# Mixers' gates moved by DMA and transposed on TensorE as fp32r instead of float32

## The chip, the cores and the metric

The kernel runs on one core of a Trainium2 chip. A core has five engines with instruction queues of their own, which run in order and wait for each other through semaphores: TensorE (PE in the profile; its weight loads are PEld), VectorE (DVE), ScalarE (ACT), GpSimd (POOL) and SyncE (SP). Sixteen DMA engines move data between memories. The metric is the device time of one execution in microseconds.

## What is computed

A stack of two blocks over 256 rows of 1024 columns, all in float32. The first block has two mixers, a sliding window attention and a block attention; the second has two hybrid layers. Only the mixers of the first block have the gates that this change touches. A mixer is, cut down:

```python
proj = h @ w_in                                   # q, k, v, z
o = attention(rope(q), rope(k), v)                # softmax(...) @ v
o = o.reshape(B, S, MIX_WIDTH) * jax.nn.silu(z)   # the gate
h = h + o @ w_out[i]
```

## The kernel before

Rows are cut into M = 2 tiles of P = 128; the 1024 columns into KD = 8 tiles of 128. Every weight matrix arrives in chunks of 1 MB (`raw`, three buffers, loaded by SP). ScalarE rounds a chunk to fp32r (`hi`, L1547), VectorE takes the rest (`lo`, L1159), and TensorE multiplies three times, hi by hi, lo by hi and hi by lo (L1371). fp32r is the kind of float32 operand that TensorE takes in one pass. A chunk of 4 x 128 x 512 is 24 products of 128x512. The split of a chunk is queued two chunks ahead of its products.

What each engine does and in which order is one list of steps, made by `build_schedule`; each engine walks it and emits its own part of every step. There is no planner: a step's place in the code is its place in each queue.

A mixer (`mixer_ab`) projects q, k, v, then the two halves of z (512 columns each), then multiplies by `w_out`. Its attention is cut into stages `attention(sc, n)`, n = 0 to 5, laid between the chunks; the names `att(n)` stand for them. Stage 3 has, on ScalarE, the last eight exponentials of the scores (`attn_prob`, L1734 and L1736).

The gate, for each half of z and each m:

- `ev_z` (ScalarE, L1657) makes silu(z) from PSUM as `attn_z`. `den` (VectorE) makes 1 / softmax sum, `dens`.
- `gate` (GpSimd, L1901) multiplies both into `quarter`, 128 x 512 in float32. There are two quarter buffers, shared with other work.
- `turn_gate` (TensorE, L1250) transposes the quarter as four blocks of 128x128 into a PSUM bank (`bank<-cst,quarter`; `cst` holds the identity), since the attention's result `attn_o` stands transposed. VectorE multiplies `attn_o` by it (L2243).
- `split_o` rounds the product into `oT_hi` (ScalarE, L1769) and `oT_lo` (VectorE, L2248), from which the output product reads.

So there are 2 mixers x 2 halves x 2 row tiles = 8 quarters and 32 transposes of this kind. Half 0's two quarters are turned together, in the middle of the second chunk of z's second half. Half 1's are turned singly, in the middle of the first and of the second chunk of the output product.

`turn_gate` and `split_o` of both halves are called here:

```python
b = halves(sc, w_in, [(D + 2 * kvw + 512, 512)], [lambda: fill_gates(sc, a, 0, za)], att(3),
           [lambda: turn_gates(sc, a, 0)])
...
out_product(sc, w_out, KD, {
    0: (att(5), [lambda: turn_gates(sc, a, 1, 0)]),
    1: ([lambda: turn_gates(sc, a, 1, 1)], ())}, mid)
```

Of the kernel before, what the change touches and what calls it, by code (L numbers as in the profile page):

```python
# [22 lines left out]
F32 = mybir.dt.float32  # L23
F32R = mybir.dt.float32r
# [6 lines left out]
S, D, P = 256, 1024, 128  # L31
# [397 lines left out]
def halves(sc, w, cols, a=(), b=(), c=()):  # L429

    blk = sc.block(sum(cw for _, cw in cols))
    project_chunk(sc, w, cols, [0, 1, 2, 3], blk, True, False, a, b)
    project_chunk(sc, w, cols, [4, 5, 6, 7], blk, False, True, c)
    return blk
# [75 lines left out]
def fill_gates(sc, a, half, z):  # L510


    es = a["sinks"][half] if a["kind"] == "a" else None
    den = sc.step("den", att=a, half=half, es=es)
    a["gates"][half] = [sc.quarter("gate", att=a, half=half, m=m, z=z, den=den) for m in range(M)]


def turn_gates(sc, a, half, *ms):


    turned = []
    for m in ms or range(M):
        b = sc.bank()
        oev = a["oev"][2 * half:2 * half + 2]
        s = sc.step("turn_gate", att=a, half=half, m=m, of=a["gates"][half][m], oev=oev, bank=b)
        b.freed = (s, "vector")
        sc.turned_quarter(s)
        turned.append(s)
    for s in turned:
        sc.oturned[half, s.m] = sc.step("split_o", att=a, half=half, m=s.m, of=s)  # L530


def new_attention(sc, which, heads, nkv):
    a = sc.att = {"kind": which, "heads": heads, "nkv": nkv, "scores": [], "flip": [], "pv": [], "oev": [],
                  "base": sc.heads, "tk": [], "tq": [], "gates": {}, "sinks": [], "normed": {}}
    sc.heads += heads
    if which == "h" and sc.heads == 40:
        sc.prob_readers, sc.last_pv4 = [None] * 4, [None] * 2
    return a


def mixer_ab(sc, which, w_in, w_out, nkv, mid=False):

    kvw = nkv * HD
    a = new_attention(sc, which, 16, nkv)

    def att(*ns):
        return [lambda n=n: attention(sc, n) for n in ns]

    kv = [(D, 2 * kvw)]  # L550
    b = halves(sc, w_in, [(0, 512)])
    ev = evacs(sc, b, "ev_q", j=0, kind_of=which)
    rq0 = sc.step("pool_rope" if nkv > 2 else "rope_q", j=0, kind_of=which, ev=ev)
    if nkv == 2:
        b = sc.block(2 * kvw)
        project_chunk(sc, w_in, kv, list(range(KD)), b, True, True)
    else:
        b = halves(sc, w_in, kv)
    ev = evacs(sc, b, "ev_kv", nkv=nkv, dt=None)
    kr = sc.step("rope_k", nkv=nkv, kind_of=which, ev=ev)  # L560
    if sc.heads == 32:

        bk = sc.bank()
        s = sc.step("taps", bank=bk)
        bk.freed = (s, "scalar")
    b = halves(sc, w_in, [(512, 512)], (), [lambda: turn_queries(sc, a, 0, rq0)], [lambda: turn_keys(sc, a, kr)])
    ev = evacs(sc, b, "ev_q", j=1, kind_of=which)
    rq1 = sc.step("pool_rope", j=1, kind_of=which, ev=ev)
    sc.low_later = True
    sc.goes_on(att(0))  # L570

    def queries():
        turn_queries(sc, a, 1, rq1)
        if mid:
            sc.step("mid_load", before=a["tq"][-1])

    b = halves(sc, w_in, [(D + 2 * kvw, 512)], (), att(1), [queries])
    sc.goes_on(att(2))
    za = evacs(sc, b, "ev_z", j=0, kind_of=which)
    if mid:  # L580
        sc.gain_now = sc.gain(None)
        sc.gain_now["made"] = sc.step("mid_gain")
    b = halves(sc, w_in, [(D + 2 * kvw + 512, 512)], [lambda: fill_gates(sc, a, 0, za)], att(3),
               [lambda: turn_gates(sc, a, 0)])
    sc.goes_on(att(4))
    zb = evacs(sc, b, "ev_z", j=1, kind_of=which)
    fill_gates(sc, a, 1, zb)
    out_product(sc, w_out, KD, {
        0: (att(5), [lambda: turn_gates(sc, a, 1, 0)]),
        1: ([lambda: turn_gates(sc, a, 1, 1)], ())}, mid)  # L590


# [313 lines left out]
def half_of(c, half):  # L906
# [13 lines left out]
    "scores": ("tensor", "vector", "scalar"),   # L920
    "flip4": ("tensor", "vector"), "scalar_flip4": ("tensor", "scalar"), "pv4": ("tensor",),
    "oev4": ("scalar",), "vector_oev4": ("vector",), "o_split": ("scalar", "vector"), "over": ("vector",),
    "p_norm_scalar": ("scalar",), "p_norm_vector": ("vector",), "sink": ("vector", "scalar"), "den": ("vector",), "gate": ("gpsimd",),
    "turn_gate": ("tensor", "vector"), "split_o": ("scalar", "vector"), "pool_rope": ("gpsimd",),
    "soft1": ("vector", "scalar"), "soft2": ("vector", "scalar"), "soft3": ("vector",),
    "sums": ("tensor", "vector", "scalar"), "conv": ("tensor", "scalar", "vector"), "conv_silu": ("scalar",),
# [10 lines left out]
def build(nc, t):  # L937
# [14 lines left out]
    def at(name, shape, dt, where=None):  # L952
        size = math.prod(shape[1:]) * (2 if dt == BF16 else 4)
        size = -(-size // LINE) * LINE
        if where is None:
            where = place[0]
            place[0] += size
        else:
            at.end = max(at.end, where + size)
        return nc.alloc_sbuf_tensor_at(name, shape, dt, offset=where), where + size  # L960

    def keep(name, shape, dt=F32):
        return at(name, shape, dt)[0]
# [6 lines left out]
    warm, _ = at("warm", [P, 1], BF16, place[0] - 2 * 12 * S * 4)  # L970
    gain_rows8, _ = at("gain_rows8", [KD, P], F32, place[0] - 2 * 12 * S * 4 + 1024)
    gain_cols, _ = at("gain_cols", [P, KD], F32, place[0] - 2 * 12 * S * 4 + 1536)
    raw = [keep(f"raw{i}", [P, CH]) for i in range(RAW)]
    hi = [keep(f"hi{i}", [P, CH], F32R) for i in range(SPLIT)]
    lo = [keep(f"lo{i}", [P, CH], F32R) for i in range(SPLIT)]
# [113 lines left out]
    taps_in, e = at("taps_stage", [P, P], F32, e)  # L1089
    angle, e = at("trig_stage", [P, M, 2, 8], F32, e)  # L1090
    sine, e = at("trig_stage2", [P, M, 2, 8], F32, e)
    turns, _ = at("trig_stage3", [P, M, 2, 8], F32, e)

    mid_rows = [at(f"mid_row{i}", [P, D], F32, A["q_at"] + 4 * D * i)[0] for i in range(2)]
    assert max(place[0], at.end) <= 229344, (place[0], at.end)
# [21 lines left out]
    warm_up = nc.alloc_semaphore("warm_up")  # L1117
    picks_made = nc.alloc_semaphore("picks_made")
    gain_in = nc.alloc_semaphore("gain_in")
    setup_dve = nc.alloc_semaphore("setup_vector")  # L1120
    setup_act = nc.alloc_semaphore("setup_scalar")
    out_done = [nc.alloc_semaphore(f"out_done{m}") for m in range(M)]
# [3 lines left out]
    def ended(eng, step, who):  # L1126

        eng.wait_ge(sem[step.kind, who], step.i + 1)
# [119 lines left out]
    def _(pe):  # L1248
# [26 lines left out]
        for s in sc.steps:  # L1275
# [184 lines left out]
                                                pt[:, p0 + r * QC + S:p0 + r * QC + QC], start=False, stop=True)  # L1460
                last.then_inc(sem["pv4", "tensor"], 1)
            elif s.kind == "turn_gate":
                ended(pe, s.of, "gpsimd")
                bank = freed(pe, s.bank)
                for i in range(4):
                    last = transpose(bank[:, i * P:(i + 1) * P], quarter[s.of.buf][:, i * P:(i + 1) * P])
                last.then_inc(sem["turn_gate", "tensor"], 1)
            elif s.kind == "sums":
                ended(pe, s.before, "vector")
# [69 lines left out]
    def _(act):  # L1539
# [38 lines left out]
        for s in sc.steps:  # L1578
# [12 lines left out]
            elif s.kind == "turn":  # L1591
                act.wait_ge(sem["turn", "tensor"], s.i + 1)
                bank = psum[4 + s.bank.at]
                if s.dst == "h":
                    out = hT[0][:, s.k0:s.k0 + 2, :].rearrange("p k t -> p (k t)")
                    done(nc.scalar.activation(out, bank[:, :], ACT.Copy), s)
                else:
                    dst = (xT if s.dst == "x" else oT)[0]
                    done(nc.scalar.activation(dst[:, s.k0:s.k0 + 4, s.m * P:(s.m + 1) * P],
                                              bank[:, :].rearrange("p (k t) -> p k t", k=4), ACT.Copy), s)  # L1600
            elif s.kind == "piece":
                piece(s.i)
            elif s.kind == "x_split":
# [805 lines left out]
```

## Time and profile before

| | us |
|---|---|
| median of 3 runs | 851.33 |
| range of the runs | 851.17 to 851.60 |
| profiled execution, its time | 851.23 |
| profiled execution, its span | 849.4 |

Busy shares of the span: TensorE 99%, VectorE 74%, ScalarE 63%, GpSimd 24%. The granted clock of TensorE is at full speed over the whole span. The span is the stretch from the first to the last instruction; 1.8 us of the execution's time lie around it.

### The profile page before, as it was taken

The numbers are of one execution on the slowest core, as the hardware profiler recorded it, in microseconds if no ns is written. First come the engines' busy times: TensorE is split into PE (matmuls) and PEld (weight loads), VectorE is DVE, ScalarE is ACT, GpSimd is POOL, SyncE is SP. The second block draws the span as 40 slices with busy tenths as digits, with TensorE's granted clock in tenths as the row PEclk, the third lists the DMA queues.
The fourth block names the chain that finished last, engine by engine and source line by source line (L and its number), as shares of the span: only waits on it lengthen the run. The fifth ranks groups of instructions, "written<-read, shape, count | busy, mean of one in ns | idle before, by whom it ended". The sixth has DMA issues, their size and how long they took to land.

```text
span 849.4 us, 13003 instructions
## 1 busy us (share of the span) xinstructions
PE 842.3 (99%) x4635; PEld 707.1 (83%) x4635; DVE 624.3 (74%) x1109; ACT 535.6 (63%) x1035; POOL 202.3 (24%) x175
## 2 busy tenths in 40 slices
PE   9999999999999999999999999999999999999997
PEld 6888888788888888888888888888888888888885
DVE  6867865778776798688888546576797688888544
ACT  8677466856896864655556434787874655665533
POOL 0221053110152420033333000152330043334000
PEclk9999999999999999999999999999999999999999
DMA  9823563446534435665655565444347566565631
GB/s 329 287 82 124 174 204 117 150 149 188 172 119 146 149 131 192 206 199 182 186 194 196 200 198 175 152 148 149 104 145 222 176 198 198 184 181 185 227 116 50
DMA packets 94307, 146.20 MB, mean 172 GB/s; under 512 B 5924, under 2 KB 54564, under 8 KB 94244
## 3 DMA queue, kind: packets, MB, share of 16 engines
q1 hardware_dynamic: 92212, 139.58, 50.1%
q0 software_dynamic: 1296, 4.72, 1.6%
q10 hardware_dynamic: 736, 1.07, 0.3%
q8 instruction: 38, 0.62, 0.3%
q14 instruction: 25, 0.20, 0.1%
HBM read 144.32 MB, written 1.05 MB: 171 GB/s over the span
## 4 chain that ended last, share of the span: by engine, by line
PE 99%; DMA 0%; ACT 0%; DVE 0%; SPq 0%; issue 0%; DVEq 0%; ACTq 0%
PE bank L1371 58%; PE bank L1324 17%; PE bank L1327 9%; PE bank L1250 6%; PE bank L1528 2%; PE bank L1456 1%; PE bank L1432 1%; PE bank L1429 1%; PE bank L1459 1%; PE bank L1271 0%; PE bank L1266 0%; DMA h<-in_x 0%; PE bank L1518 0%; PE bank L1535 0%; PE bank L1269 0%; PE bank L1496 0%
## 5 line engine op out<-in xcount | busy, mean ns | idle before, releaser
L1159 DVE TENSOR_TENSOR lo<-raw,hi 128x1024 fp32r<-128x1024 f32 x242 | 308.8, 1293 | 106.3 <-ACT hi L1547 106.0
L1547 ACT ACTIVATE hi<-raw 128x1024 fp32r<-128x1024 f32 (+1 forms) x258 | 269.3, 1061 | 138.1 <-PE bank L1371 70.8
L1371 PE MATMUL bank<-hi,xT 128*128 128x512 f32 (+2 forms) x800 | 251.9, 386 | 0.0
L1371 PEld LDWEIGHTS bank<-hi,xT 128*128 128x128 f32 x800 | 147.2, 188 | 30.8 <-issue 4.3
L1371 PE MATMUL bank<-lo,xT 128*128 128x512 f32 (+2 forms) x400 | 151.1, 378 | 0.0
L1324 PE MATMUL bank<-xT,hi 128*128 128x512 f32 x640 | 149.5, 390 | 0.0
L1324 PEld LDWEIGHTS bank<-xT,hi 128*128 128x128 f32 x640 | 118.7, 188 | 24.3 <-DVE quarter L2143 0.5
L1371 PE MATMUL bank<-hi,hT 128*128 128x512 f32 x348 | 107.7, 389 | 0.0
L1371 PEld LDWEIGHTS bank<-lo,xT 128*128 128x128 f32 x400 | 75.4, 189 | 12.1
L1327 PE MATMUL bank<-xT,lo 128*128 128x256 f32 x640 | 80.5, 283 | 0.0
L1327 PEld LDWEIGHTS bank<-xT,lo 128*128 128x128 f32 x640 | 79.4, 191 | 1.4
L1371 PEld LDWEIGHTS bank<-hi,hT 128*128 128x128 f32 x348 | 65.3, 188 | 13.5
L1371 PE MATMUL bank<-lo,hT 128*128 128x512 f32 x174 | 67.7, 389 | 0.0
L1371 PE MATMUL bank<-hi,oT_hi 128*128 128x512 f32 x160 | 66.1, 413 | 0.0
L1859 POOL TENSOR_TENSOR f_up<-f_up,row_scale 128x256 f32<-128x256 f32 x40 | 46.4, 1182 | 73.3 <-DVE f_up L2154 73.3
L1371 PE MATMUL bank<-hi,oT_lo 128*128 128x512 f32 x160 | 62.6, 391 | 0.0
L1371 PE MATMUL bank<-lo,oT_hi 128*128 128x512 f32 x160 | 62.4, 390 | 0.0
L1159 POOL TENSOR_TENSOR lo<-raw,hi 128x1024 fp32r<-128x1024 f32 x16 | 39.0, 2445 | 61.4 <-ACT hi L1547 61.4
L1859 POOL TENSOR_TENSOR f_gate<-f_gate,row_scale 128x256 f32<-128x256 f32 x40 | 33.9, 869 | 79.2 <-DVE f_gate L2154 79.2
L2302 DVE SCALAR_TENSOR_TENSOR hyb_acc<-bank,taps,hyb_acc 128x255 f32<-128x255 f32 (+2 forms) x72 | 29.0, 474 | 15.8 <-ACT hyb_acc L1794 15.8
L1371 PEld LDWEIGHTS bank<-lo,hT 128*128 128x128 f32 x174 | 32.7, 188 | 6.8
L1371 PEld LDWEIGHTS bank<-hi,oT_hi 128*128 128x128 f32 x160 | 30.1, 188 | 6.7 <-issue 1.3
(285 smaller groups left out, 1085.2 us busy)
## 6 DMA issues: line engine op xcount, KB each, us to landing
raw<-in_w_in SPq DMA_DIRECT2D x26, 1024.0 KB, 5.0
raw<-in_w_down SPq DMA_DIRECT2D x22, 1024.0 KB, 4.9
raw<-in_w_out SPq DMA_DIRECT2D x20, 1024.0 KB, 5.1
raw<-in_w_gate SPq DMA_DIRECT2D x20, 1024.0 KB, 5.3
raw<-in_w_up SPq DMA_DIRECT2D x20, 1024.0 KB, 5.3
raw<-in_w_in_b SPq DMA_DIRECT2D x10, 1024.0 KB, 5.0
raw<-in_w_in_a SPq DMA_DIRECT2D x7, 1024.0 KB, 7.7
raw<-in_w_in_a SPq DMA_DIRECT2D x8, 256.0 KB, 5.3
```

What stands on the lines that cost most here:

```text
L1159: return engine.tensor_tensor(lo[r][:, cols], raw[c.i % RAW][:, cols], hi[r][:, cols].bitcast(F32), ALU.subtract)
L1250: return nc.tensor.transpose(out, in_, ident)
L1324: last = nc.tensor.matmul(both, hi[r][:, still], xx[:, k, :, :], start=first, stop=last_one, skip_group_check=c.i % 2 == 1)
L1327: last = nc.tensor.matmul(bank[:, 0:S], lo[r][:, still], xT[0][:, k, :], start=first, stop=last_one, skip_group_check=c.i % 2 == 1)
L1371: last = nc.tensor.matmul(bank[:, 0:wd], still[a], mv[r][:, off:off + wd], start=c.first and i == 0 and j == 0, stop=(c.last or c.closes a ...
L1429: nc.tensor.matmul(bank[:, 0:P], q[r:r + 64, hd // 2, 0:P], k[r:r + 64, kv, 0:P], start=True, stop=True)
L1432: nc.tensor.matmul(bank[:, P:QC], q[r:r + 64, hd // 2, P:S], k[r:r + 64, kv, 0:S], start=True, stop=True).then_inc(sem["scores", "tensor"], 1)
L1456: nc.tensor.matmul(bank[64 * r:64 * r + 64, o0:o0 + S], v[:, 0, kv + r, :], pt[:, p0 + r * QC:p0 + r * QC + S], start=True, stop=False)
L1528: last = nc.tensor.matmul(bank[:, c0:c0 + HD], Hb[f"MT{s.decay.of.i % 4}"][:, i, :], Hb["xg"][:, s.m, hh * HD:(hh + 1) * HD], start=True, ...
L1547: nc.scalar.activation(hi[c.i % SPLIT][:, cols], raw[c.i % RAW][:, cols], ACT.Copy)\
L1859: nc.gpsimd.tensor_tensor(x[:, :], x[:, :], row_scale[:, :], ALU.mult)\
L2302: ins = stt(acc[:, tap:S], x[:, 0:S - tap], cw[:, 3 - tap, ct:ct + 1], acc[:, tap:S], ALU.mult, ALU.add)
```

## The change

A new step `gate_move` stands between `gate` and `turn_gate`. ScalarE's queue waits for the gate of GpSimd and issues a DMA of 256 KB, from the quarter into one of two tiles `moved`, word for word. `moved` is declared fp32r; the DMA goes through a float32 view, so no bit changes. TensorE waits for the landing, and transposes `moved` as fp32r into a bank that is viewed as fp32r, with an identity in fp32r (`same`), which ScalarE makes once, ahead of the first move. `moved` lies in the part of `oT_hi` that the mixers don't use. The moves of half 0 are queued behind attention stage 3, those of half 1 ahead of stage 5.

```diff
+def move_gates(sc, a, half):
+    a["moved"][half] = [sc.step("gate_move", of=a["gates"][half][m]) for m in range(M)]
...
-    b = halves(..., [lambda: fill_gates(sc, a, 0, za)], att(3),
+    b = halves(..., [lambda: fill_gates(sc, a, 0, za)], att(3) + [lambda: move_gates(sc, a, 0)],
                [lambda: turn_gates(sc, a, 0)])
...
-        0: (att(5), [lambda: turn_gates(sc, a, 1, 0)]),
+        0: ([lambda: move_gates(sc, a, 1)] + att(5), [lambda: turn_gates(sc, a, 1, 0)]),
...
             elif s.kind == "turn_gate":
-                ended(pe, s.of, "gpsimd")
+                if s.i == 0:
+                    pe.wait_ge(same_made, 1)
+                pe.wait_ge(gate_moved[s.of.i % 2], 16 * (s.of.i // 2 + 1))
                 bank = freed(pe, s.bank)
                 for i in range(4):
-                    last = transpose(bank[:, i * P:(i + 1) * P], quarter[s.of.buf][:, i * P:(i + 1) * P])
+                    last = nc.tensor.transpose(bank[:, i * P:(i + 1) * P].bitcast(F32R),
+                                               moved[s.of.i % 2][:, i * P:(i + 1) * P], same[:, :])
...
+            elif s.kind == "gate_move":
+                if s.i == 0:
+                    nc.scalar.activation(same[:, :], ident, ACT.Copy).then_inc(same_made, 1)
+                ended(act, s.of, "gpsimd")
+                if s.i >= 2:
+                    act.wait_ge(sem["turn_gate", "tensor"], s.i - 1)
+                act.dma_start(moved[s.i % 2][:, :].bitcast(F32), quarter[s.of.buf][:, :])\
+                   .then_inc(gate_moved[s.i % 2], 16)
```

ScalarE's queue at the end of attention stage 3 of the first mixer (half 0), before. Names are out<-in, the semaphores waited for are in brackets:

```order
L1734 ACTIVATE attn_prob,totals<-bank,shift 128x128 [waits flip4_tensor,scores_vector]
L1736 ACTIVATE attn_prob,totals<-bank,shift 128x256
L1547 ACTIVATE hi_60<-raw_57 128x1024 [waits chunk_tensor,raw_in1]
L1769 ACTIVATE oT_hi<-attn_o 128x4x128 [waits turn_gate_vector] x2
L1547 ACTIVATE hi_60<-raw_57 128x1024
```

The same place in the change:

```order
L1754 ACTIVATE attn_prob,totals<-bank,shift 128x128 [waits flip4_tensor,scores_vector]
L1756 ACTIVATE attn_prob,totals<-bank,shift 128x256
L1615 ACTIVATE same<-cst 128x128
L1619 DMA moved_56<-quarter_67 128x512 [waits gate_gpsimd]
L1619 DMA moved_57<-quarter_68 128x512 [waits gate_gpsimd]
L1559 ACTIVATE hi_62<-raw_59 128x1024 [waits chunk_tensor,raw_in1]
L1789 ACTIVATE oT_hi<-attn_o 128x4x128 [waits turn_gate_vector] x2
L1559 ACTIVATE hi_62<-raw_59 128x1024
```

The two moves stand behind the exponentials and ahead of the split of the next chunk.

TensorE's queue at the turning of half 0, first mixer, before and in the change:

```order
L1371 MATMUL bank<-hi_61,xT 128x512
L1250 MATMUL bank<-cst,quarter_65 128x128 [waits scalar_flip4_scalar,gate_gpsimd]
L1250 MATMUL bank<-cst,quarter_65 128x128 x3
L1250 MATMUL bank<-cst,quarter_66 128x128 [waits flip4_vector,gate_gpsimd]
L1250 MATMUL bank<-cst,quarter_66 128x128 x3
L1371 MATMUL bank<-hi_61,xT 128x512 [waits x_split_vector]
```

```order
L1380 MATMUL bank<-hi_63,xT 128x512
L1477 MATMUL bank<-same,moved_56 128x128 [waits scalar_flip4_scalar,gate_moved0,same_made]
L1477 MATMUL bank<-same,moved_56 128x128 x3
L1477 MATMUL bank<-same,moved_57 128x128 [waits flip4_vector,gate_moved1]
L1477 MATMUL bank<-same,moved_57 128x128 x3
L1380 MATMUL bank<-hi_63,xT 128x512 [waits x_split_vector]
```

The place in the queue is the same; the wait for GpSimd has become one for the landing.

ScalarE's queue at half 1 of the first mixer, before and in the change:

```order
L1547 ACTIVATE hi_61<-raw_58 128x1024 [waits chunk_tensor,raw_in2]
L1752 ACTIVATE attn_o<-bank 128x512 [waits pv4_tensor] x2
L1547 ACTIVATE hi_61<-raw_58 128x1024
L1769 ACTIVATE oT_hi<-attn_o 128x4x128 [waits turn_gate_vector]
```

```order
L1559 ACTIVATE hi_63<-raw_60 128x1024 [waits chunk_tensor,raw_in2]
L1619 DMA moved_56<-quarter_67 128x512 [waits turn_gate_tensor,gate_gpsimd]
L1619 DMA moved_57<-quarter_68 128x512 [waits turn_gate_tensor,gate_gpsimd]
L1772 ACTIVATE attn_o<-bank 128x512 [waits pv4_tensor] x2
L1559 ACTIVATE hi_63<-raw_60 128x1024
L1789 ACTIVATE oT_hi<-attn_o 128x4x128 [waits turn_gate_vector]
```

The copies of `attn_o` and half a split now stand behind two waits for GpSimd.

## Rows read from the trace of the kernel before

**Rows 1.** The page: busy times of the engines, and the chain that ended last.

```profile
PE 842.3 (99%) x4635; PEld 707.1 (83%) x4635; DVE 624.3 (74%) x1109; ACT 535.6 (63%) x1035; POOL 202.3 (24%) x175
...
PE 99%; DMA 0%; ACT 0%; DVE 0%; SPq 0%; issue 0%; DVEq 0%; ACTq 0%
```

**Rows 2.** Timeline of PE, half 0 of both mixers: start, length (us), line, count.

```profile
69.96 1.04 PE L1250 MATMUL bank<-cst,quarter 128*128 128x128 f32 x8
70.75 0.47 PE L1371 MATMUL bank<-hi,xT 128*128 128x512 f32 x1
...
170.56 1.04 PE L1250 MATMUL bank<-cst,quarter 128*128 128x128 f32 x8
171.35 0.47 PE L1371 MATMUL bank<-hi,xT 128*128 128x512 f32 x1
```

**Rows 3.** Timeline of ACT, end of attention stage 3, both mixers.

```profile
70.49 0.24 ACT L1736 ACTIVATION_READ_ACCUMULATOR attn_prob<-bank,shift 128x1 f32 x1
70.58 1.10 ACT L1547 ACTIVATE hi<-raw 128x1024 fp32r<-128x1024 f32 x1
...
171.10 1.10 ACT L1547 ACTIVATE hi<-raw 128x1024 fp32r<-128x1024 f32 x1
```

**Rows 4.** Timeline of POOL, gates of the first mixer, half 0 and half 1.

```profile
62.18 2.06 POOL L1901 TENSOR_TENSOR quarter<-attn_z,dens 128x512 f32<-128x512 f32 x2 [16.76 <-ACT attn_z L1657]
78.88 3.04 POOL L1901 TENSOR_TENSOR quarter<-attn_z,dens 128x512 f32<-128x512 f32 x2 [14.64 <-ACT attn_z L1657]
```

**Rows 5.** DMA issues: tile, queue, count, KB each, median us from issue to landing.

```profile
raw<-in_w_in_b SPq DMA_DIRECT2D x10, 1024.0 KB, 5.0
out<-result SPq DMA_DIRECT2D x3, 256.0 KB, 2.1
raw<-in_w_in SPq DMA_DIRECT2D x2, 64.0 KB, 5.1
```

**Rows 6.** Line L1709, a DMA issued by ACT: the issue's ns, its landing.

```profile
L1709 ACTq DMA_DIRECT2D out<-result x1: 360/360/360, 846.5 to 846.5; - x1
...
DMA to landing us min/median/max: 2.1/2.1/2.1
```

**Rows 7.** Stretches of 1 us: busy us (instructions), clock, DMA share, GB/s.

```profile
71.00:72.00 1.00, 1.00 (x6) 0.79 (x6) 1.00 (x2) 0.68 (x1) 0.00 (x0) 1.00 0.00 0
82.00:83.00 1.00, 1.00 (x6) 0.82 (x5) 0.78 (x1) 0.19 (x1) 0.00 (x0) 1.00 1.07 416
```

**Rows 8.** Groups of PE and PEld by shape: busy us, mean ns | idle before.

```profile
L1371 PE MATMUL bank<-hi,hT 128*128 128x512 f32 x348 | 107.7, 389 | 0.0
L1353 PE MATMUL bank<-hi,hT 128*128 128x256 f32 x8 | 1.6, 282 | 0.0
L1250 PE MATMUL bank<-cst,quarter 128*128 128x128 f32 x152 | 22.4, 272 | 0.0
...
L1371 PEld LDWEIGHTS bank<-hi,hT 128*128 128x128 f32 x348 | 65.3, 188 | 13.5
L1250 PEld LDWEIGHTS bank<-cst,quarter 128*128 128x128 f32 x152 | 18.7, 140 | 4.4
L1528 PEld LDWEIGHTS bank<-hyb_xg,hyb_MT 128*128 128x128 f32 x128 | 15.2, 192 | 0.3
```

**Rows 9.** Timeline of PE: products in bfloat16, and 64-wide ones in float32.

```profile
286.38 0.62 PE L1518 MATMUL bank<-csum,picks 112*128 112x128 bf16 x8
...
289.62 1.89 PE L1528 MATMUL bank<-hyb_xg,hyb_MT 128*128 128x64 f32 x16
```

**Rows 10.** Timelines of PE, ACT and DVE, half 1 of the first mixer.

```profile
83.39 0.60 PE L1250 MATMUL bank<-cst,quarter 128*128 128x128 f32 x4
86.58 0.60 PE L1250 MATMUL bank<-cst,quarter 128*128 128x128 f32 x4
89.79 0.39 PE L1371 MATMUL bank<-hi,oT_hi 128*128 128x512 f32 x1
...
80.64 0.60 ACT L1752 ACTIVATE attn_o<-bank 128x512 f32<-128x512 f32 x1 [0.50 <-PE bank L1459]
...
85.41 0.69 DVE L2248 TENSOR_TENSOR oT_lo<-attn_o,oT_hi 128x512 fp32r<-128x512 f32 x1 [0.70 <-ACT oT_hi L1769]
```

**Rows 11.** PE at the end of the run, and its warm-up at the start.

```profile
843.14 0.28 PE L1353 MATMUL bank<-hi,hT 128*128 128x256 f32 x1
...
847.00:849.40 2.40, 0.00 (x0) 0.57 0.60 212
...
0.93 3.52 PE L1255 MATMUL bank<-warm 128*128 128x512 bf16 x8 [0.93 <-DVE warm L2017]
```

More of the change, by code:

```diff
@@ L524, in turn_gates @@
         oev = a["oev"][2 * half:2 * half + 2]
-        s = sc.step("turn_gate", att=a, half=half, m=m, of=a["gates"][half][m], oev=oev, bank=b)
+        s = sc.step("turn_gate", att=a, half=half, m=m, of=a["moved"][half][m], oev=oev, bank=b)
         b.freed = (s, "vector")
@@ L534, in new_attention @@
     a = sc.att = {"kind": which, "heads": heads, "nkv": nkv, "scores": [], "flip": [], "pv": [], "oev": [],
-                  "base": sc.heads, "tk": [], "tq": [], "gates": {}, "sinks": [], "normed": {}}
+                  "base": sc.heads, "tk": [], "tq": [], "gates": {}, "moved": {}, "sinks": [], "normed": {}}
     sc.heads += heads
@@ L582, in mixer_ab @@
         sc.gain_now["made"] = sc.step("mid_gain")
[L583 removed]
+    b = halves(sc, w_in, [(D + 2 * kvw + 512, 512)], [lambda: fill_gates(sc, a, 0, za)], att(3) + [lambda: move_gates(sc, a, 0)],
                [lambda: turn_gates(sc, a, 0)])
@@ L922 @@
     "oev4": ("scalar",), "vector_oev4": ("vector",), "o_split": ("scalar", "vector"), "over": ("vector",),
-    "p_norm_scalar": ("scalar",), "p_norm_vector": ("vector",), "sink": ("vector", "scalar"), "den": ("vector",), "gate": ("gpsimd",),
+    "p_norm_scalar": ("scalar",), "p_norm_vector": ("vector",), "sink": ("vector", "scalar"), "den": ("vector",), "gate": ("gpsimd",), "gate_move": (),
     "turn_gate": ("tensor", "vector"), "split_o": ("scalar", "vector"), "pool_rope": ("gpsimd",),
@@ L972, in build @@
     gain_cols, _ = at("gain_cols", [P, KD], F32, place[0] - 2 * 12 * S * 4 + 1536)
+    moved = [at(f"moved{i}", [P, 512], F32R, place[0] - (2 * 12 - 8) * S * 4 + 2048 * i)[0] for i in range(2)]
     raw = [keep(f"raw{i}", [P, CH]) for i in range(RAW)]
@@ L1091, in build @@
     sine, e = at("trig_stage2", [P, M, 2, 8], F32, e)
-    turns, _ = at("trig_stage3", [P, M, 2, 8], F32, e)
+    turns, e = at("trig_stage3", [P, M, 2, 8], F32, e)
+    same, e = at("same", [P, P], F32R, e)
     mid_rows = [at(f"mid_row{i}", [P, D], F32, A["q_at"] + 4 * D * i)[0] for i in range(2)]
@@ L1119, in build @@
     gain_in = nc.alloc_semaphore("gain_in")
+    gate_moved = [nc.alloc_semaphore(f"gate_moved{i}") for i in range(2)]
+    same_made = nc.alloc_semaphore("same_made")
     setup_dve = nc.alloc_semaphore("setup_vector")
```

## The prediction, made before the change was run

> **What bounds the kernel now.** I read the page first. TensorE is busy for 842.3 of 849.4 us, and the chain that ended last lies on it for 99% [rows 1]. So every nanosecond of TensorE's own work counts, in both directions, and so does every wait that is put on it: it has no later idle time in which to take a delay back. All other engines have spare time, and what they do counts only where TensorE ends up waiting for it.
>
> Then the timelines, at the places where gates are turned. In half 0 TensorE starts the eight transposes at 69.96 us, and the next product starts at 70.75; in the second mixer these are 170.56 and 171.35 [rows 2]. No idle time stands before either. The gates have long been there: GpSimd starts the first mixer's two at 62.18 and is done after 2.06 us, at 64.24 [rows 4]. The reader should see that this is 5.7 us of slack in front of TensorE, enough for a DMA, if the DMA is issued as soon as the gate is ready. The change doesn't do that. It queues the move on ScalarE behind the last exponentials of attention stage 3, and ScalarE is at them until 70.58 to 70.73 [rows 3], which is after TensorE has arrived at the transposes.
>
> **What the transposes cost, and what is saved.** Eight transposes take 1.04 us, of which the last takes its whole 272 ns: (1.04 - 0.27) / 7 = 0.110 us apart [rows 2, 8]. As fp32r, the product itself should be shorter. A product in fp32r takes 389 ns at 512 columns and 282 at 256, 107 ns for 256 columns or 0.42 ns for one; the float32 transpose of 128 columns takes 272, where this line gives 282 - 54 = 228 [rows 8]. So an fp32r pass streams the identity in about 54 ns, and a float32 transpose in about twice that. The lower end of the spacing is what bfloat16 shows: eight products of 128 columns in 0.62 us, some 0.056 apart [rows 9]. The upper end comes from weight loads. A load in float32 or fp32r for an ordinary product takes 188 to 192 ns, one for a transpose 140 [rows 8]; and 64-wide products, each behind a load of 192 ns, are (1.89 - 0.27) / 15 = 0.108 us apart although they stream only 64 columns [rows 9] (0.27 for the last, as for a transpose). If an fp32r transpose loads its weights like an ordinary fp32r product, it stays at 0.108 and nothing is saved; if it loads like a transpose, it comes to 0.056. I take 0.056, since the load is of a transpose in both kernels and the row of transposes is the nearer one, and keep 0.110 for the range. The saving is 4 x 0.054 = 0.21 us a quarter. For the four quarters of half 1 it is 0.85 us in all, on the path in full. In half 0 it is inside the sum below.
>
> The Trainium skill has a rule that speaks against the change: "TensorE: Matmul & The Clock Gate", Terms, says that trn2's loads and products have a transpose mode which makes float32 4 times faster, so the float32 transpose would already be the quick form. The rows here show a transpose at 272 ns, against 228 for one fp32r pass, so something would be left to save. By the rule alone the saving is nil.
>
> **What the waits cost, half 0.** A move of 256 KB that ScalarE issues costs its queue 0.36 us [rows 6], and 256 KB take 2.1 us from issue to landing [rows 5]. These are writes to memory outside the core, the nearest rows; the moves stay inside. No other traffic is there to disturb them: the DMA engines are idle from 71 to 72 us [rows 7]. 1 MB takes 5.0 us [rows 5], and the engines move about 416 GB/s when busy [rows 7], so 256 KB are 0.64 us of their work. The second move, issued 0.36 us behind the first, lands 0.64 behind it.
>
> - First mixer. ScalarE is free at 70.58 [rows 3]. The identity's copy, once, is 128x128; I put it at 0.25 us. The first move is issued at 70.83 and lands at 72.93; the second lands at 73.57. TensorE turns the first quarter while it waits for the second, then needs 0.05 to notice and 0.22 to turn it. The next product starts at 73.85, not 70.75: +3.1 us.
> - Second mixer. No copy. Issued at 171.10 [rows 3], landings at 173.20 and 173.84, next product at 174.12, not 171.35: +2.8 us.
>
> Together +5.9 us. Behind TensorE nothing gives it back: its wait holds the remaining twelve products of the chunk and all that follows. No row shows a move inside the core, so below the 2.1 I keep an end of 1.4, two thirds of it, with both streams at once: the second landings are then at 72.59 and 172.86, and the stalls 2.1 + 1.8 = 3.9. The page "DMA: Bandwidth & Descriptors" of the Trainium skill, Anatomy of one DMA, gives a fixed 2.0 us plus bytes over 436 GB/s, an estimate of 2.6 us for 256 KB; with it each stall would be 0.5 longer and the time 857.2.
>
> **Half 1.** The gates start at 78.88 and end after 3.04 us, the first near 79.9 and the second at 81.92 [rows 4]. The first move is issued near 79.95, lands near 82.1, and is wanted at 83.39; the second is issued at 81.95, lands near 84.1, and is wanted at 86.58 [rows 10]. No stall, with 1.3 and 2.4 us to spare. What is new is that ScalarE stands in its queue until 81.92. Behind it are the two copies of `attn_o`, of which the second began at 80.64 [rows 10], and half a split of 1.05 us. They would end at about 83.5 and 84.6. VectorE's `oT_lo` for m = 0, which ended at 86.1, then ends near 87.9. The products that read it start at 89.79 [rows 10]. So the delay is hidden by 1.9 us; without that cover it would cost up to the 1.8 us by which `oT_lo` is late, in each mixer. The eight issues (8 x 0.36 = 2.9 us) lie on ScalarE, which is at 63% [rows 1], and for half 0 inside TensorE's stall.
>
> **The sum.** +5.9 (two stalls) - 0.85 (half 1's transposes) = +5.0 us. Against the profiled execution, 851.23 + 5.0 = 856.2; that execution is 0.1 us from the median of the runs.
>
> **The rivals.**
>
> *The transposes don't get faster.* The stalls remain; -0.85 falls away, and in each stall the last quarter takes 0.44 instead of 0.22: +6.3, 857.5. This is also the case in which the change does not do what it says. For it: the skill's rule above, and the loads of 188 ns. Against it: the load's row of 140 for transposes.
>
> *The clock falls in the stalls.* TensorE does nothing for nearly 3 us twice. The trace has one such place, the end of the run: the last product starts at 843.14 and ends at 843.4, and the clock's mean in 847.0 to 849.4 is 0.57 [rows 11], so it fell to the lower level (1.2 GHz) near 847.3, 3.9 us after the last work. That is longer than my stalls, but one case is little. The price: at the start eight products of 512 columns take 3.52 us at the lower level, about 0.42 us each [rows 11], where an fp32r one is 0.23 at the upper; until the clock rises some 1.6 us are lost. With both stalls, +3.2: 859.4.
>
> *The moves of half 1 land late.* A load of 1 MB is under way then: DMA is at 1.07 of its engines in 82 to 83 us [rows 7]. A small transfer queued with a large one took 5.1 us [rows 5]. With that, the first move lands at 85.05 against 83.39, and the same in the second mixer where I allow 1 us: +2.7, 858.9.
>
> *Faster after all.* The mechanism: the wait on the landing costs nothing since the moves are in before TensorE comes, and the transposes' saving is all that is left. The place is half 0 of each mixer. It decides at the issue: the move would have to leave ScalarE before about 67.6 us, 2.1 + 0.2 ahead of 69.96. The gates are there in time [rows 4], but ScalarE's queue runs in order, and the exponentials ahead reach to 70.73 [rows 3]. Price: 8 quarters x 0.21 = 1.7, so 849.5, faster by 0.2%. I see nothing that lets it happen, unless a wait of TensorE elsewhere gives the stalls back; there is none [rows 1].
>
> **How the numbers follow.** Chances: forecast 0.55 (856.2, own range 854.3 to 857.2), transposes not faster 0.2 (857.5), clock 0.12 (859.4), late landings 0.08 (858.9), faster 0.02, and 0.03 for stalls so short that it ends within 0.2%. 0.2%, or 1.7 us, is about what a measurement of this kernel can tell from no change. The range reaches from the short stalls, 851.23 + 3.9 - 0.85 = 854.3, to the clock case, 859.4, with which it takes in the late landings too; only what lies below 854.3 and mixtures of the rivals are left out. Slower by over 0.2% has 0.95.
>
> **What would show it.** Right: TensorE idle for 2.5 to 3 us before the transposes of `moved` in half 0, released by a DMA, twice; none in half 1; eight transposes no longer 0.110 apart; landings 2 to 2.7 us after issues near 70.8 and 171.1 (the second shifted by the first stall). Wrong: a stall in half 1, a granted clock under 1 after a stall, transposes at 272 ns as before, or idle time of TensorE elsewhere, as before the output product's third chunk, where `oT_lo` would be late.

## The result, and the profile after

| | before | after |
|---|---|---|
| median of the runs | 851.47 us (851.17 to 851.64) | 864.67 us (863.0 to 865.04) |
| profiled execution | 851.23 us | 864.48 us |
| its span | 849.4 us | 862.6 us |
| mean granted clock | 0.999 | 0.994 |

The ratio is 1.0152, with an interval of 1.014 to 1.0164: slower by 13.2 us. I had forecast slower by 5.0.

The page of the changed kernel, which answers to [rows 1]: busy times, and the chain that ended last.

```profile
PE 847.6 (98%) x4635; PEld 710.2 (82%) x4635; DVE 624.7 (72%) x1109; ACT 535.2 (62%) x1036; POOL 202.2 (23%) x175
...
PE 95%; DMA 2%; ACT 1%; DVE 0%; issue 0%; POOL 0%; POOLq 0%; ACTq 0%; DVEq 0%
```

Two things stand in it. The chain now passes through DMA and ACT for 3%, so TensorE waits. And TensorE is *busy* for 5.3 us more (847.6 against 842.3) with the same 4635 products. A wait doesn't make products longer; a lower clock does.

The timeline of PE at the four places where it waits. The bracket is the idle time before the group and what ended it.

```profile
71.90 0.50 PE L1477 MATMUL bank<-same,moved 128*128 128x128 f32 x4 [1.73 <-ACT same L1615]
72.60 0.54 PE L1477 MATMUL bank<-same,moved 128*128 128x128 f32 x4 [0.19 <-DMA moved<-quarter]
72.97 0.51 PE L1380 MATMUL bank<-hi,xT 128*128 128x512 f32 x1
...
89.18 0.54 PE L1477 MATMUL bank<-same,moved 128*128 128x128 f32 x4 [1.88 <-DMA moved<-quarter]
...
179.45 0.54 PE L1477 MATMUL bank<-same,moved 128*128 128x128 f32 x4 [1.48 <-DMA moved<-quarter]
180.20 0.54 PE L1477 MATMUL bank<-same,moved 128*128 128x128 f32 x4 [0.21 <-DMA moved<-quarter]
...
195.81 0.60 PE L1477 MATMUL bank<-same,moved 128*128 128x128 f32 x4 [2.48 <-DMA moved<-quarter]
```

The first line names ACT's copy `same`, but that ended at 70.99 (below), 0.9 us earlier. The wait is for several semaphores, and the last to come was the landing of the move. So there are four stalls, not two: half 0 and half 1 of both mixers. Half 1's second quarter (93.98 us) is in time.

Stretches of the same kernel: busy us and count per engine, then the granted clock, DMA share, GB/s.

```profile
71.90:73.00 1.10, 0.91 (x9) 0.77 (x9) 0.56 (x1) 0.03 (x1) 0.00 (x0) 1.00 0.66 84
73.00:76.40 3.40, 3.40 (x11) 2.70 (x10) 2.18 (x4) 2.21 (x3) 0.00 (x0) 0.54 0.79 298
76.40:79.00 2.60, 2.60 (x19) 2.29 (x18) 0.79 (x2) 0.53 (x1) 0.00 (x0) 0.95 0.00 0
...
90.10:93.50 3.40, 3.40 (x10) 2.67 (x9) 2.27 (x3) 1.58 (x2) 0.00 (x0) 0.53 0.81 243
...
180.40:184.00 3.60, 3.60 (x22) 3.06 (x22) 2.34 (x4) 2.22 (x3) 0.00 (x0) 1.00 0.98 263
196.00:199.20 3.20, 3.20 (x11) 2.65 (x11) 2.06 (x3) 1.58 (x2) 0.00 (x0) 0.52 0.94 320
```

After three of the four stalls the clock is at its lower level (1.2 GHz); after the one at 179.45 it stays at 1.00. The count of products shows it too: 11 in 3.4 us there, 22 in 3.6 us here.

**Where the 13.2 us are.** I took the start of a product and subtracted the start of the same product in the trace of before. This difference only moves at these places:

| place | stall | clock after it |
|---|---|---|
| half 0, first mixer | +2.16 | +1.57 |
| half 1, first mixer | +2.05 | +1.58 |
| half 0, second mixer | +1.96 | none |
| half 1, second mixer | +2.68 | +1.54 |
| sum | +8.85 | +4.69 |

The stall is what the difference has gained at the first ordinary product behind the transposes; the clock's part is what it gains after that, until it stands still. The stalls are larger than the brackets, because a product normally starts 0.23 us behind its forerunner, while a bracket counts from the end of the forerunner 0.39 us after its start. The four places give 13.5 us; some 0.3 come back elsewhere, 0.1 of them at half 1's second quarters, where fp32r transposes run without a stall. Behind the last place the difference stays at +13.2 to +13.3 to the end: as good as nothing is given back.

The timeline of ACT and its queue in half 0, which answers to [rows 3]:

```profile
69.40 0.49 ACT L1756 ACTIVATE attn_prob<-bank,shift 128x256 f32<-128x256 f32 x1
69.50 0.51 ACTq L1619 DMA_DIRECT2D moved<-quarter  x1
...
70.06 0.61 ACTq L1619 DMA_DIRECT2D moved<-quarter  x1
...
70.64 0.35 ACT L1615 ACTIVATE same<-cst 128x128 fp32r<-128x128 f32 x1
```

The summary of the tile `moved`, which answers to [rows 6, 8]: ns min/median/max, first and last start, and the landings after their issue.

```profile
L1477 PEld LDWEIGHTS bank<-same,moved x32: 138/140/157, 71.9 to 200.8; 128*128 128x128 f32 x32
L1477 PE MATMUL bank<-same,moved x32: 222/249/308, 71.9 to 200.8; 128*128 128x128 f32 x32
L1619 ACTq DMA_DIRECT2D moved<-quarter x8: 472/473/608, 69.5 to 190.9; - x8
...
DMA to landing us min/median/max: 2.3/3.3/6.9
```

ScalarE issued both moves while exponentials that stand ahead of them in the program were still running, and the first one 1.1 us before the copy `same` began, which also stands ahead of it. That is why half 0's stalls are shorter than forecast. And landings take from 2.3 to 6.9 us: the long ones are half 1's. The chain that ended last, in half 1 of the first mixer (start, length, what), and the load beside it on SP's queue:

```profile
83.75 5.39 DMA moved<-quarter
89.14 0.04 issue
89.18 0.54 PE bank L1477 x4
```

```profile
82.77 7.21 SPq L1224 DMA_DIRECT2D raw<-in_w_in_b  x2
```

The trace's DMA view by queue says how the load holds up the move. In it q1 is SP's queue and q10 is the one of the moves; the numbers are packets, MB and share of the 16 engines. The first line is the stretch from 83.5 to 87.1 us, the other two that from 87.1 to 89.5.

```profile
q1 hardware_dynamic: 449, 0.92, 83.9%
...
q10 hardware_dynamic: 288, 0.52, 57.5%
q1 hardware_dynamic: 79, 0.13, 14.5%
```

The first move is issued at 83.75, but up to 87.1 only the load's packets run: 449 of its 528. Then come both moves together (288 packets) and the load's last 79. In half 0, with no load under way, the packets of a move start 1.2 us behind its issue; here it is 3.4 us. So the engines do not share themselves out between the two: the small transfer stands behind nearly the whole of the large one.

### The profile page after: what moved, and what is told of

The parts are those of the page before. It is cut to its first block, busy times and chain, and to the rows that moved or that the text cites. A ratio compares the mean times of both kernels' runs of the same rounds, so it can differ in the third digit from the quotient of the medians.

```text
span 862.6 us, 13018 instructions
## 1 busy us (share of the span) xinstructions
PE 847.6 (98%) x4635; PEld 710.2 (82%) x4635; DVE 624.7 (72%) x1109; ACT 535.2 (62%) x1036; POOL 202.2 (23%) x175
## 4 chain that ended last, share of the span: by engine, by line
PE 95%; DMA 2%; ACT 1%; DVE 0%; issue 0%; POOL 0%; POOLq 0%; ACTq 0%; DVEq 0%
PE bank L1380 56%; PE bank L1333 17%; PE bank L1336 9%; PE bank L1259 5%; DMA moved<-quarter 2%; PE bank L1540 2%; PE bank L1441 1%; PE bank L1465 1%; PE bank L1438 1%; PE bank L1280 0%; PE bank L1275 0%; PE bank L1530 0%; PE bank L1547 0%; PE bank L1278 0%; PE bank L1264 0%; PE bank L1468 0%
## 5 line engine op out<-in xcount | busy, mean ns | idle before, releaser
L1380 PEld LDWEIGHTS bank<-hi,hT 128*128 128x128 f32 x348 | 65.3, 188 | 13.5
L1380 PE MATMUL bank<-hi,oT_lo 128*128 128x512 f32 x160 | 63.6, 397 | 0.0
L1380 PEld LDWEIGHTS bank<-hi,oT_lo 128*128 128x128 f32 x160 | 30.9, 193 | 6.9
```

What stands on the lines that cost most here:

```text
L1380: last = nc.tensor.matmul(bank[:, 0:wd], still[a], mv[r][:, off:off + wd], start=c.first and i == 0 and j == 0, stop=(c.last or c.closes a ...
```

## The experiments

My theory after this reading had three parts. (1) Half 0 is late because the move is issued late. (2) Half 1 is late because SP's 1 MB load, issued 1 us ahead, holds up the move. (3) TensorE's clock falls after such stalls, at about 1.5 us a time (the expectations below reckon with 1.7). The rivals: ScalarE or its queue is what makes the moves slow; the longer busy time has another cause than the idleness; the fp32r transposes themselves gain or lose more than I think. Line numbers shift by a few between the kernels.

### TensorE kept at work during the wait

```diff
+FILL = 7
...
+    if s.of.i % 2 == 0:
+        for _ in range(FILL):
+            nc.tensor.matmul(bank[:, :], xT[0][:, 0, 0:P], hi[live[0]][:, 0:512], start=True, stop=True)
     pe.wait_ge(gate_moved[s.of.i % 2], 16 * (s.of.i // 2 + 1))
```

> The change, with seven fp32r products of 512 columns (7 x 0.227 = 1.6 us) on TensorE ahead of its wait for the first move of each pair, into the bank that the transposes then overwrite. Theory 1 (13.2 us = about 8 of four stalls plus 5.1 of three falls of the clock, each 3.42 us at the lower level, 1.7 lost): the moves land when they landed, but TensorE isn't idle for them, so the clock stays at 1.00 for the whole span and the time is 864.7 - 5.1 = 859.6. Theory 2 (the slow products after a stall come from something else that the stall brings, such as a loss of order between the queues): the low stretches stay and the time is 864.7 or a little over.

858.60 us (858.55 to 858.77), ratio 1.0085 [1.0069, 1.01]: 6.1 us less than the changed kernel, for extra work on the engine that bounds it. The timeline of PE in half 0:

```profile
70.02 1.75 PE L1477 MATMUL bank<-hi,xT 128*128 128x512 f32 x7
71.96 0.50 PE L1482 MATMUL bank<-same,moved 128*128 128x128 f32 x4 [0.19 <-DMA moved<-quarter]
```

Stretches behind the first mixer's two places and the second's first:

```profile
71.80:75.00 3.20, 2.82 (x17) 2.39 (x18) 2.43 (x4) 1.84 (x4) 0.00 (x0) 1.00 0.70 216
87.00:90.50 3.50, 3.44 (x18) 2.63 (x17) 2.54 (x4) 1.58 (x2) 0.00 (x0) 1.00 0.38 97
175.00:180.00 5.00, 4.71 (x26) 3.70 (x25) 3.58 (x5) 3.34 (x6) 0.00 (x0) 1.00 0.78 280
```

The transposes start no earlier (71.96 against 71.90), but the clock holds at 1.00 where it was 0.53 to 0.54, in these stretches and in all others of the two mixers. This shows part 3: idleness costs clock beyond its own length. Of the 6.1 us 4.7 are the clock's by the table above; the rest is that landings in half 1 took 5.2 us at most instead of 6.9, which this experiment didn't aim at: by the products' offsets half 1's stalls are 1.8 and 1.5 us here, where they were 2.1 and 2.7.

### Each half alone

In both kernels the other half's gates are turned from `quarter` in float32, as before the change. The diff is that of half 0 alone; the other has `half != 1`, and a wait of its moves counts other transposes.

```diff
 def move_gates(sc, a, half):
+    if half != 0:
+        a["moved"][half] = a["gates"][half]
+        return
```

> Only half 0's gates are moved by DMA and turned as fp32r; half 1's as before. Theory 1: the stalls of half 0 alone, 2.2 + 1.9 us, one fall of the clock (1.7) or two (3.4), 16 transposes at 0.085 us apart and not 0.109 (-0.4): 851.4 + 5.4 = 856.8, or 858.5 with two falls. Theory 3 (the four stalls aren't independent, the first one makes the later ones): with half 1 unmoved nearly all of the loss goes, or stays.

> Only half 1's gates are moved by DMA and turned as fp32r; half 0's as before. Theory 1: the stalls of half 1 alone, 2.2 + 2.8 us since the moves land 5 to 7 us after their issue beside a load of 1 MB, two falls of the clock (3.4), 16 transposes at 0.085 us (-0.4): 851.4 + 8.0 = 859.4. The extra of half0 and of this together is that of the change, 13.2. Theory 3 (the stalls of half 1 come from the delay of half 0): no stall here, and 851.0.

Half 0 alone took 855.69 us (855.62 to 855.77), ratio 1.005 [1.0033, 1.0067], with no fall of the clock; half 1 alone 856.91 (856.73 to 857.76), 1.0066 [1.0051, 1.0081], its profiled run the one of 857.76. Half 0 alone, timeline of PE:

```profile
72.41 0.50 PE L1486 MATMUL bank<-same,moved 128*128 128x128 f32 x4 [1.74 <-ACT same L1624]
73.09 0.53 PE L1486 MATMUL bank<-same,moved 128*128 128x128 f32 x4 [0.18 <-DMA moved<-quarter]
```

The stretch after it:

```profile
73.50:77.00 3.50, 3.50 (x21) 2.95 (x20) 2.27 (x5) 2.22 (x3) 0.00 (x0) 1.00 0.87 290
```

Its landings:

```profile
DMA to landing us min/median/max: 2.3/2.4/2.5
```

Half 1 alone, its landings, and a stretch in the second mixer:

```profile
DMA to landing us min/median/max: 4.0/5.7/7.3
```

```profile
189.40:192.80 3.40, 3.40 (x13) 2.68 (x12) 2.40 (x3) 1.57 (x2) 0.00 (x0) 0.56 0.77 286
```

So the stalls of half 0 are worth 4.1 us without any fall of the clock, and those of half 1 some 5.1 (2.0 and 3.1 by the products' offsets, as in the table above), with a fall worth 1.6 in the profiled run. I had expected one or two falls in the first kernel and two in the second: the profiled runs have none and one. 4.1 + 5.3 = 9.4 against 13.2 for both. The missing 3.8 are not shown piece by piece, since only one run of each kernel has a trace. The mean granted clock, which every run lists, was 0.998 and 0.999 in the runs of half 0 alone, as before the change, but 0.996 and 0.997 in all of half 1 alone. So those runs too had most likely one fall each and shorter stalls than the profiled one. Then 3.1 of the 3.8 are the two falls more of the whole kernel's trace, and 0.7 are longer stalls.

### The moves kept, the transposes in float32

```diff
-    moved = [at(f"moved{i}", [P, 512], F32R, ...
+    moved = [at(f"moved{i}", [P, 512], F32, ...
-    last = nc.tensor.transpose(bank[...].bitcast(F32R), moved[...], same[:, :])
+    last = transpose(bank[...], moved[...])
```

> The moves stay, but the transposes are of float32 again, from the moved tile. It measures what fp32r gives. By the trace after (0.085 us apart): 32 x 0.024 = 0.8 us, of which 0.2 lie inside stalls, so 864.7 + 0.6 = 865.3. By the prediction's 0.056: 864.7 + 1.3 = 866.0. If the kind is worth nothing: 864.7.

863.59 us (861.93 to 865.38), ratio 1.0143 [1.0128, 1.0159]. It should have been slower than the changed kernel by what fp32r saves, and came out 1.1 us faster, with two stretches at the lower clock in its trace (from 88.8 and from 194.6 us, both at half 1's stalls) against three. The scatter of its runs, 3.4 us, is larger than the thing to be measured, so this run decides nothing on the transposes. The same edit on top of the kernel that keeps TensorE at work has no falls in the way:

> The moves and the seven products in front of each pair of transposes are as in the kernel that fills the waits (858.60), but the moved tiles are float32 and so are the transposes. No stretch at the lower clock is expected, so the difference is the transposes' kind alone. By the spacing that the changed kernel's trace shows (0.085 us against 0.109), 32 transposes take 32 x 0.024 = 0.8 us less as fp32r: this kernel then takes 859.4. By the 0.054 us that I had predicted for each it would be 860.3. If the kind gives nothing, 858.6.

859.18 us (859.0 to 859.59), ratio 1.0094 [1.0078, 1.0109], against 858.60: fp32r saves 0.6 us. Each was timed beside runs of before of its own (851.59 and 851.44), so 0.6 may be 0.7; the single runs of the two kernels don't overlap, but the intervals of their ratios do. Its transposes, and the changed kernel's above, differ by 24 ns in length:

```profile
L1260 PE MATMUL bank<-cst,moved x32: 270/273/330, 72.1 to 195.5; 128*128 128x128 f32 x32
```

### The load held back until the move has landed

```diff
     if s.kind == "chunk" and s.i + RAW < len(chunks):
+        if s.i in held:
+            sp.wait_ge(gate_moved[0], 16 * held[s.i])
         load(chunks[s.i + RAW])
```

> As the changed kernel, but the 1 MB load that SP issues just ahead of half 1's moves waits for the first move to land. Theory: the moves of half 1 land 4 to 7 us after their issue only because that load's packets stand ahead of them. Then they land about 2.4 us after issue, as in half 0, both stalls of half 1 are gone and so are their falls of the clock (5.3 us in the kernel that moves half 1 alone), and half 0's stalls stay, with or without a fall of the clock: 864.7 - 5.3 = 859.4, down to 855.7 if no fall is left (the kernel that moves half 0 alone). Rival: the late landing comes from ScalarE or its queue; then half 1's moves land as late as before and the time stays at 864. Second rival: the load held back by 3 us becomes the bound of the next products, which would wait for it: 864 or more, with PE waiting for a raw tile.

859.66 us (858.73 to 860.3), ratio 1.0097 [1.0084, 1.0111]. Its landings:

```profile
DMA to landing us min/median/max: 2.3/2.5/2.8
```

The timeline of PE, at half 1's first quarter and behind it:

```profile
86.82 0.46 PE L1484 MATMUL bank<-same,moved 128*128 128x128 f32 x4
...
106.38 0.50 PE L1387 MATMUL bank<-hi,xT 128*128 128x512 f32 x1 [1.33 <-DVE xT L2104]
```

Two stretches, each behind a stall of half 0:

```profile
72.00:75.40 3.40, 3.22 (x12) 2.60 (x12) 2.67 (x4) 2.21 (x3) 0.00 (x0) 0.56 0.00 0
177.90:181.20 3.30, 3.30 (x11) 2.74 (x12) 2.48 (x4) 2.21 (x3) 0.00 (x0) 0.54 0.00 0
```

This shows part 2. The diff tells SP to wait for the first move's landing before it issues the load. The issuing engine, its queue and the move are the same as in the changed kernel; only the load was taken from beside it, and the longest landing went from 6.9 to 2.8 us. No bracket stands before half 1's transposes. What remains is half 0 with a fall of the clock behind each stall, a new wait of 1.33 us at 106.38, and one of 0.35 at 201.88. Both are for VectorE: the load that was held back is late at ScalarE's split, VectorE's part of the split follows it, and VectorE comes late to what TensorE needs. That was my second rival, in a small form.

### The moves issued by SP, early

```diff
+    if s.kind == "gate_move":
+        ended(sp, s.of, "gpsimd")
+        ...
+        sp.dma_start(moved[s.i % 2][:, :].bitcast(F32), quarter[s.of.buf][:, :])...
```

This stands in SP's program; ScalarE has none of it. In the first kernel both halves are moved so, half 1's ahead of the load; in the second only half 0's, and half 1's are turned as before the change.

> The moves are issued by SP, right after the gates are made and half 1's ahead of its next 1 MB load, and ScalarE has none. Theory: all that the change costs is a move issued too late. Half 0's gates are ready at 62.2, 7.8 us ahead of the transposes; even a landing 5 to 7 us later is in time or 1 us late. Half 1's gates are ready at 82.7 and 85.7 and need 2.3 us with no load ahead. Then there is no stall and no fall of the clock, and the transposes give 32 x 0.024 = 0.8 us: 850.8. Rival: a wait that takes their place, SP's loads held behind the moves' waits for their gates (up to 3 us each, four times): raw tiles come late and the time is 853 to 860, with PE waiting for a load.

> Only half 0's gates are moved, by SP as soon as GpSimd has made them, 6 us and more ahead of their transposes; half 1's are turned as float32 as in the kernel before. Theory: a move issued early costs nothing, and sixteen fp32r transposes give 16 x 0.024 = 0.4 us: 851.0 to 851.1 against 851.4. Rival: SP's wait for the gates delays a load that is needed and the time is over 851.8, with PE waiting behind a raw tile.

The first took 852.62 us (852.12 to 852.83), ratio 1.0013 [1.0004, 1.0021]. PE waits at no transpose, but it has the new wait of my rival, at one place: SP stands behind half 1's gates, the load is issued at 82.84, and ScalarE waits for it. VectorE waits for ScalarE in turn, works almost without a pause from there on, and makes its copy to `xT` too late for TensorE. The timelines of SP, of ACT, of DVE and of PE, a line each:

```profile
82.84 0.54 SPq L1225 DMA_DIRECT2D raw<-in_w_out  x1
```

```profile
88.28 1.06 ACT L1566 ACTIVATE hi<-raw 128x1024 fp32r<-128x1024 f32 x1 [2.71 <-DMA raw<-in_w_out]
```

```profile
89.37 1.23 DVE L1169 TENSOR_TENSOR lo<-raw,hi 128x1024 fp32r<-128x1024 f32 x1 [3.07 <-ACT hi L1566]
```

```profile
103.49 0.50 PE L1387 MATMUL bank<-hi,xT 128*128 128x512 f32 x1 [1.37 <-DVE xT L2099]
```

By the products' offsets that wait is worth 1.6 us; without it the kernel would be at 851.0.

The second took 851.06 us (850.87 to 851.45), ratio 0.9996 [0.9987, 1.0004], as the theory said: no wait, and 0.3 us less than the 851.38 of before beside it, which is within the interval of no difference. Its first pair of transposes with the product behind them:

```profile
70.27 0.80 PE L1492 MATMUL bank<-same,moved 128*128 128x128 f32 x8
70.90 0.46 PE L1389 MATMUL bank<-hi,xT 128*128 128x512 f32 x1
```

Its landings:

```profile
DMA to landing us min/median/max: 2.2/2.4/3.2
```

This shows part 1: the same move of the same tile for the same transposes costs nothing when it is issued at 63.6, and 4.1 us (in two mixers) when it is issued at 69.5 to 70. The issuer has changed as well, from ScalarE to SP, but a move takes no less time for that: 2.2 to 3.2 us from issue to landing, against 2.3 to 2.5. What differs is when it is issued.

### No move at all

GpSimd writes the gate into the fp32r tile itself, and ScalarE has nothing to issue.

```diff
-    q = quarter[s.buf][:, :].rearrange("p (a d) -> p a d", d=HD)
+    q = moved[s.i % 2][:, :].rearrange("p (a d) -> p a d", d=HD)
...
```

TensorE waits for the gate, and GpSimd for the transposes that read its tile before.

> No move at all: GpSimd writes the gate into the fp32r tile itself and so rounds it (the gates' last bits are left out, so the result differs a little), and ScalarE has no DMA to issue. Transposes are fp32r as in the changed kernel. Theory: the transposes' kind alone is worth 32 x 0.024 = 0.8 us: 850.8 against 851.6. By my prediction's 0.054 us each it would be 850.0 (0.85 us for the half on the path that I counted, 1.7 for both). If the kind gives nothing on the path, 851.6. Rival: GpSimd's product into an fp32r tile takes longer than the 2.06 and 3.04 us of before, and half 1's gates come late.

850.66 us (850.29 to 851.13), ratio 0.9992 [0.9983, 1.0001], 0.78 us less than before. By the products' offsets 0.54 of it lies at the transposes; the rest lies at no one place. GpSimd takes no longer than before (62.29 for 2.06 us, 78.84 for 3.04, as in [rows 4]):

```profile
62.29 2.06 POOL L1918 TENSOR_TENSOR moved<-attn_z,dens 128x512 fp32r<-128x512 f32 x2 [16.76 <-ACT attn_z L1672]
78.84 3.04 POOL L1918 TENSOR_TENSOR moved<-attn_z,dens 128x512 fp32r<-128x512 f32 x2 [14.49 <-ACT attn_z L1672]
```

The timeline of PE, half 0 of the first mixer:

```profile
70.08 0.80 PE L1477 MATMUL bank<-same,moved 128*128 128x128 f32 x8
70.71 0.46 PE L1380 MATMUL bank<-hi,xT 128*128 128x512 f32 x1
```

Eight transposes and the start of the next product are 0.63 us apart instead of 0.79 [rows 2]. It is the fastest of all the kernels here, by a difference that lies just at the edge of its interval.

### The whole change and half 0 once more, side by side

> The changed kernel once more, beside half 0 alone, on one chip. Its median was 864.67 where it was first timed; with four stalls (8.4 us by the offsets of its products) and each fall of the clock worth 1.7 us, no fall gives 859.6, two give 863.0, three give 864.7. If the number of falls goes by the run and not by the kernel, single runs should differ by steps of about 1.7 us.

> Only half 0's gates are moved, once more. Where it was first timed it took 855.69 with no fall of the clock; the kernel that holds the load back has the same two stalls there and showed two falls, on another chip. If the falls are a matter of the chip or the moment, this one takes 855.7 in some runs and 857.4 or 859.1 in others; if something in the rest of the kernel decides them, 855.7 in every run again.

The changed kernel took 863.45 us, in single runs 862.34, 862.68, 864.22 and 864.29, ratio 1.0143 [1.0127, 1.0158]; its profiled run (862.68) has four stalls and two falls. Half 0 alone took 856.9, in single runs 855.32, 855.85, 856.90, 856.91 and 856.96, ratio 1.0058 [1.0045, 1.0071]; its profiled run is the 855.32, with no fall. Both kernels' times stand in two clusters, 1.7 and 1.3 us apart, and the mean granted clock goes with them: 0.998 in the two shorter runs of half 0 alone and 0.996 in the other three, 0.994 to 0.995 and 0.993 in those of the changed kernel. The same stall, 1.74 us before the transposes at 71.9, was followed by a fall in the changed kernel's first trace and in the kernel that holds the load, and by none here and in the changed kernel's second trace. So whether a stall of this size costs the clock is a matter of the run; only the profiled runs show it directly, for the others it is inferred from the steps. In the seven traces of kernels that make such stalls and don't fill them, a fall went with all four brackets of 2.4 us and more, and with six of the sixteen from 1.5 to 2.0 us.

## Why the prediction was wrong

The direction was right and the size was not: 851.23 + 5.0 = 856.2, with 859.4 as the upper end, against 864.7. By its own steps:

- **What bounds the kernel**: right. Each wait put on TensorE went into the time, and next to nothing was given back in 650 us behind the last stall.
- **Half 0, +5.9 forecast**: the mechanism was right, the size was not. The offsets give 2.16 and 1.96, and half 0 alone 4.1. The step that failed is "the first move is issued at 70.83", behind ScalarE's last exponential. It was issued at 69.50. I had taken ScalarE's queue to hold a DMA until the instructions ahead of it are done; it issued it 1.1 us before the copy that stands ahead of it began. The landing, 2.3 to 2.5 us after the issue, was close to the 2.1 of [rows 5], and the second was 0.7 behind the first, as forecast. An issue took 0.47 to 0.61 us, not 0.36. The copy `same`, put at 0.25 us ahead of the move, took 0.35 and stood behind it. The 2.6 us that the prediction takes from the Trainium skill ("DMA: Bandwidth & Descriptors", Anatomy of one DMA) is a fit on DMAs that GpSimd issues; ScalarE's took 0.1 to 0.3 less.
- **Half 1, "No stall, with 1.3 and 2.4 us to spare"**: the second step that failed, and the costliest: 4.7 us of stalls, and two of the three falls of the clock behind them. The moves were issued when forecast, 1.1 us behind the gate's start at 82.67, but the first landed 5.4 us later and, in the second mixer, 6.9. It was the rival with 0.08, whose row (5.1 us for a small transfer beside a large one, [rows 5]) was the nearer one: a load was under way [rows 7]. I took the row for an idle queue instead. The two stalls came to 2.1 and 2.7 us (2.0 and 3.1 with half 1 alone) where the rival had 1.7 and 1.0. Holding the load back removed them, so the load is the cause, and the packets show how: the moves' stood behind the load's.
- **ScalarE blocked behind the gate**: as forecast it cost nothing. The copies of `attn_o` waited 2.81 us, and no product that reads `oT_lo` did.
- **The clock, put at nothing in the sum and a rival with 0.12**: the third step that failed. Its price was right (1.6 forecast, 1.5 to 1.6 measured), its chance and its number were not. I weighed the one place where TensorE stood idle in the trace, the end of the run, where the clock fell 3.9 us after the last work [rows 11], as if shorter idleness were safe. In the changed kernel it fell after brackets of 1.7 to 2.5 us, two or three times in four stalls, and in the one that holds the load once after 1.49. And with half 1's stalls there were four places for it, not two.
- **The transposes, -1.7 over all 32**: right in sign. The spacing went from 0.099 us (0.79 / 8) to 0.079 (0.63 / 8), a saving of 0.02 each and 0.5 to 0.8 us over all, not 0.054 and 1.7. The step that failed is the lower end of the spacing, taken from products in bfloat16 [rows 9]: by the prediction's own measure, (0.80 - 0.25) / 7, fp32r transposes are 0.079 apart, not 0.056. The product behind them also starts later, 0.08 us after the last transpose where it was 0.02. The load of 140 ns did stay, and a transpose of 249 ns is 24 shorter, not 44. The Trainium skill ("TensorE: Matmul & The Clock Gate", Terms) says that the transpose mode makes float32 four times faster, by which nothing would be left to save; the kernel without moves, 0.78 us faster than before, speaks against that here, if by little.

The sum with the measured terms: stalls 8.85 and clock 4.69, less 0.3 that comes back elsewhere, give 13.2 in the profiled run, the saving of half 0's transposes already inside the stalls. The forecast had 5.9 - 0.85. Half 0 alone was thus over-priced by 1.8 us, and what broke the forecast are half 1's stalls and the clock. The two rivals that I priced apart, late landings and the clock, came true together, and the late landings added to the clock's price, since each is one more stall for it to fall in; my upper end of 859.4 held each of them alone.

## What to carry to other kernels

A copy through DMA in front of the bounding engine cost nothing here when it was issued 3.4 us and more ahead with no large load queued just before it, and was dear otherwise: 256 KB from ScalarE landed 2.3 to 2.8 us after the issue alone and 3.7 to 7.3 beside a 1 MB load. Look at who issues the move, what stands ahead of it there, and which load is issued in the same 2 us, before pricing the work it saves. And price each new idle stretch of TensorE twice, once for its length and once, as a chance, for the 1.5 to 1.6 us that the lower clock behind it cost here.

## What the runs showed of the hardware

- A DMA that ScalarE issues can leave before the ACTIVATEs ahead of it in the program: issue at 69.50, while the copy that stands ahead of it began at 70.64.
- The move beside a 1 MB load was late by more than its share of the engines. The load alone lands in 5.0 us [rows 5] and the move alone in 2.3; issued 1 us behind the load, the move took 5.4, and none of its packets ran before 449 of the load's 528 had started. The run without the load (2.8 at most) says that the load is the cause. The Trainium skill ("DMA: Bandwidth & Descriptors", Queues, rings and completion order) says that an engine goes round between the queues it has work for and changes over only at the end of a packet, typically of 9 to 17 descriptors and at most 64. If a row of the trace (2 KB) is one descriptor, the load's 512 are 32 for each of 16 engines, an estimate. By the typical packet the move would have begun when about half of the load was through, or sooner; by the largest, only behind all of it. The trace is near the second. How the descriptors were packed no run here shows.
- The granted clock fell to the lower level after brackets of 1.5 to 2.0 us in some runs and not in others, at the same place of the same kernel, and with each of the four of 2.4 to 2.9 us. What decides it stays open.
